# A norm in front of an expert layer, moved from normalized columns to token rows

## The reference, cut to what matters

```python
x = x + gt_a * (merged @ w_o)                       # the products just ahead of the change
h = rms_norm(x, g_ffn) * (1 + sc_f) + sh_f          # factor per feature, shift per feature
logits = h @ w_router + b_router
top_val, top_idx = top_k(logits, 4)                 # 4 of 32
gates = softmax(top_val)
for each expert e, for the tokens xb that chose it:
    u = xb @ w1[e] + b1[e]
    a = min(u[::2], 7) * sigmoid(1.702 * min(u[::2], 7)) * (clip(u[1::2], -7, 7) + 1)
    y += gate * (a @ w2[e] + b2[e])
x = x + gt_f * y                                    # then a last norm
```

## Time and profile before

| what | value |
|---|---|
| median of 3 runs | 1964.3 us (1964.21 to 1966.4) |
| time of the profiled execution | 1965.39 us |
| its span in the trace | 1963.8 us, so 1.6 us lie around it |
| PE / DVE / ACT busy | 94% / 42% / 31% |
| granted PE clock, mean | 0.972 |
| PE share, DMA share of the chain that ended last | 54%, 32% |
| weight transfers of the expert layer | 192 of 2048 KB, through SP |

### The profile page before, as it was taken

How to read it: one execution, slowest core, us unless ns; L and a number is a source line. 1 busy time by engine, 2 the same in 40 slices (tenths; PEclk the granted TensorE clock), 3 DMA queues, 4 the chain that set the end, 5 groups by cost and what they waited for, 6 DMA issues and landing times.

```text
span 1963.8 us, 27025 instructions
## 1 busy us (share of the span) xinstructions
PE 1840.9 (94%) x10839; PEld 1212.9 (62%) x10840; DVE 817.7 (42%) x1402; ACT 612.3 (31%) x996; POOL 27.1 (1%) x49
## 2 busy tenths in 40 slices
PE   6899998989999899999989999999999999999996
PEld 5677777988899799989964444443443443443441
DVE  4466775557864554455532221221221221221222
ACT  4455558645544445555431000000000000000001
POOL 2000000000000000000000000000000000000000
PEclk8998999999999899999969999999999999999998
DMA  6545644455565364534739999999999999999995
GB/s 198 207 169 199 232 131 127 151 164 164 187 207 177 123 216 151 172 129 143 256 151 412 429 429 428 429 429 429 428 429 429 429 428 429 429 429 428 429 429 232
DMA packets 147620, 568.62 MB, mean 290 GB/s; under 512 B 5825, under 2 KB 102185, under 8 KB 122849
## 3 DMA queue, kind: packets, MB, share of 16 engines
q1 hardware_dynamic: 139616, 536.60, 69.3%
q0 software_dynamic: 7936, 31.07, 4.5%
HBM read 566.58 MB, written 3.43 MB: 290 GB/s over the span
## 4 chain that ended last, share of the span: by engine, by line
PE 54%; DMA 32%; DVE 7%; ACT 5%; issue 2%; SPq 0%; DVEq 0%; ACTq 0%
DMA s_ring<-in_w_mlp 31%; PE banks L2034 10%; PE banks L1652 7%; PE banks L1653 7%; PE banks L1654 7%; PE banks L1798 4%; PE banks L2071 3%; PE banks L1799 2%; PE banks L2044 2%; DVE s_W L1135 2%; DVE r_w2l L1097 2%; ACT r_w2h L701 1%; PE banks L1791 1%; PE banks L1619 1%; PE banks L1793 1%
## 5 line engine op out<-in xcount | busy, mean ns | idle before, releaser
L2034 PE MATMUL banks<-s_ring,s_W 128*64 128x512 f32 x2048 | 460.8, 597 | 28.3 <-DMA s_ring<-in_w_mlp 28.3
L2034 PEld LDWEIGHTS banks<-s_ring,s_W 128*64 128x64 f32 x2048 | 139.2, 137 | 330.3 <-issue 259.2
L1037 ACT ACTIVATE s_W<-s_W 128x512 f32<-128x512 f32 x32 | 20.2, 630 | 761.7 <-DVE s_W L1535 761.7
L2071 PE MATMUL banks<-s_ring,s_W 128*64 128x512 f32 x1024 | 226.8, 596 | 0.4 <-ACT s_W L1030 0.4
L1527 DVE TENSOR_TENSOR s_W<-banks,s_W 128x512 f32<-128x512 f32 x32 | 22.1, 691 | 461.5 <-PE banks L2071 461.5
L2071 PEld LDWEIGHTS banks<-s_ring,s_W 128*64 128x64 f32 x1024 | 73.4, 138 | 147.9 <-issue 134.1
L1097 DVE TENSOR_TENSOR r_w2l<-s_ring,r_w2h 128x1024 fp32r<-128x1024 f32 x88 | 107.6, 1223 | 114.0 <-ACT r_w2h L701 113.5
L1311 DVE TENSOR_TENSOR r_w2l<-s_ring,r_w2h 128x1024 fp32r<-128x1024 f32 x96 | 116.9, 1223 | 84.3 <-ACT r_w2h L885 84.1
L1514 DVE TENSOR_TENSOR s_W<-banks,s_W 128x512 f32<-128x512 f32 x128 | 82.1, 683 | 146.8 <-PE banks L2019 146.8
L1652 PE MATMUL banks<-r_x2h,r_w2h 128*128 128x256 f32 x448 | 130.6, 292 | 6.1 <-DVE r_x2l L1325 6.1
L2044 PEld LDWEIGHTS banks<-s_W 128*128 128x128 f32 x1024 | 120.0, 196 | 24.2 <-issue 24.2
(11 more groups left out here) (399 smaller groups left out, 3131.5 us busy)
## 6 DMA issues: line engine op xcount, KB each, us to landing
s_ring<-in_w_mlp SPq DMA_DIRECT2D x192, 2048.0 KB, 22.4
s_ring<-in_w_in SPq DMA_DIRECT2D x62, 1024.0 KB, 5.1
s_W<-in_w_ada POOLq DMA_DIRECT2D x6, 2048.0 KB, 10.0
s_ring<-in_w_ada POOLq DMA_DIRECT2D x6, 2048.0 KB, 8.7
s_ring<-in_w_ffn_gate SPq DMA_DIRECT2D x11, 1024.0 KB, 5.4
s_ring<-in_w_ffn_up SPq DMA_DIRECT2D x11, 1024.0 KB, 7.9
s_ring<-in_w_ffn_down SPq DMA_DIRECT2D x5, 2048.0 KB, 8.7
s_ring<-in_w_gate SPq DMA_DIRECT2D x8, 1024.0 KB, 5.4
```

The lines of the kernel that those rows point to most:

```text
L2034: last = mm(pb[b][64 * h:64 * h + 64, :], XgT[:, 2 * c + k, :], slot(c, 2)[:, k, 1024 * h + 512 * b:1024 * h + 512 * b + 512], start=False ...
L2071: last = mm(pb[2][64 * h:64 * h + 64, :], aT[:, k, 64 * c:64 * c + 64], slot(4 + c, 4)[:, k, 512 * h:512 * h + 512], start=c == 0 and k == ...
```

## The change

The normalized `hn` is no longer made. The router works on raw x: its weights are multiplied by the gain factor once (`wrg`), the shift's share of the logits is one row that is added to the router bias (`wrs`, `wsum`), and 1/rms is a factor per token, so it is applied after the product, on token rows. These preparations are two new steps `wrA` and `wrB` inside the `o` stage. The sum of squares is now made per token (`token_square`: x squared as the stationary side, a column of ones as the moving side), and the router product of a block (`logits`) stands between the `o` products too. ACT takes the root with Sqrt, whose table is loaded during the stage.

Raw x is turned once to token rows; ACT multiplies by the token's factor as it copies to `htok`; the turned raw x stays in banks 4 to 7 for the first sum. The gain factor and the shift are applied to the gathered tokens: the copy of bank 3 to `XgT` becomes eight activations of 64 columns, each with a factor column and a shift column read from SBUF (`modulated_rows`), in every expert. The semaphore `xg` is raised by the eighth. The four rounds that built `msk` and `gat` become one comparison over 256 columns and one reduction each, and the first sum with all that belongs to it (`first_sum`) stands behind the products of expert 0.

```diff
+                 (unit_of("o"), 1, 1, {"wrA": 1.5, "wrB": 2.5}))
...
+        def modulated_rows():
+
+            for k in range(KT):
+                last = act.activation(XgT[:, k, :], pb[3][:, 64 * k:64 * k + 64], ACT.Identity,
+                                      bias=mod_at[:, k:k + 1], scale=mod_at[:, 8 + k:9 + k])
+            return last
...
                 act.wait_ge(S["gath"], e + 1)
                 since(act, "u_mm", e * 4)
-                act.activation(XgT, pb[3].rearrange("p (a n) -> p a n", a=KT), ACT.Copy).then_inc(S["xg"], 1)
+                modulated_rows().then_inc(S["xg"], 1)
...
-        root(4, nrms, T)
-        for t in range(KT):
-            act.wait_ge(S["norm_x"], 4 * KT + t + 1)
-            act.activation(hn[:, t, :], hn[:, t, :], ACT.Identity, bias=modT[:, 24 + t:25 + t]).then_inc(S["norm_s"], 1)
+        act.wait_ge(S["norm_ms"], 5)
+        act.activation(root4, pb[3][:, 0:2], ACT.Sqrt, bias=epsc, scale=1.0 / D).then_inc(S["norm_r"], 1)
...
-        norm(4, hn, hx, nrms, gsf)
-
-        dve.wait_ge(S["moe_in"], 48)
...
+        st.do(tt(one4, iotae.unsqueeze(1).unsqueeze(1).broadcast_to([P, 2, 4, E]), at, ALU.is_equal))
+        st.wait()
+        nc.vector.tensor_reduce(msk, one4.rearrange("p t j e -> p t e j"), AX.X, ALU.add).then_inc(S["route"], 1)
...
+        def logits(k):
...
+            last = mm(pb[5][0:E, 0:T], wrg[:, k, :], hx[:, k, :], start=k == 0, stop=k == KT - 1)
...
+        def token_square(k):
+
+            if k >= 1:
+                logits(k - 1)
+            if k == KT - 1:
+                logits(k)
+            pe.wait_ge(S["norm_sq"], KT * 4 + k + 1)
+            for t in range(2):
+                last = mm(pb[3][:, t:t + 1], nsq[:, k, P * t:P * t + P], ones[:, 0:1], start=k == 0 and t == 0, stop=k == KT - 1, skip_group_check=True)
...
         expert(0, True, False)
-
+        first_sum()
         pe.wait_ge(S["acc_init"], 4)
```

More of the change, by code:

```diff
@@ L980, in _ @@
                 act.activation(v, v, ACT.Sigmoid).then_inc(S["gab_done"], 1)
+                if h == 3:
+                    act.activation(sml[:, 48:49], onec, ACT.Sqrt)
             elif s == "rgS":
@@ L1004, in _, with first_sum @@
             act.activation(half.rearrange("q (c k p) -> q c p k", c=2, k=2), pb[4 + b].rearrange("q (c p k) -> q c p k", c=2, k=2),
[L1005 to L1009, removed]
-        act.activation(gts, gts, ACT.Exp).then_inc(S["log_exp"], 1)
[L1011 to L1019, removed]
+                           ACT.Copy, scale=rtok[:, b // 2:b // 2 + 1]).then_inc(S["ht_kept"], 1)
+        act.wait_ge(S["route"], 3)
+        act.activation(gts, gts, ACT.Exp).then_inc(S["log_exp"], 1)
+        def first_sum():
+            for b in range(2):
+                act.wait_ge(S["spread"], b + 1)
+                act.activation(gtb[:, 512 * b:512 * b + 512], pb[3 - b], ACT.Copy).then_inc(S["spread_kept"], 1)
+            act.wait_ge(S["spread_kept"], 2)
+            for b in range(2):
+                v = slice(64 * b, 64 * b + 64)
+                act.activation(gty[v, :], gtb[v, 512 * b:512 * b + 512], ACT.Copy).then_inc(S["spread_kept"], 1)
+            act.wait_ge(S["gt_mm"], 1)
+            act.activation(gatT, pb[2][0:E, 0:T], ACT.Copy).then_inc(S["gt_kept"], 1)
+            for b in range(4):
+                act.wait_ge(S["h_mm"], b + 1)
+                act.activation(acc[:, b // 2, 512 * (b % 2):512 * (b % 2) + 512], pb[4 + b], ACT.Copy).then_inc(S["acc_init"], 1)
+        def modulated_rows():
[3 more added lines that the diff above has]
+            return last
         def expert(e, cur, prev):
@@ L1049, in again @@
             act.wait_ge(S["over_pe"], n * 7 + 2)
-            act.activation(XgT, pb[3].rearrange("p (a n) -> p a n", a=KT), ACT.Copy).then_inc(S["over_act"], 1)
+            modulated_rows().then_inc(S["over_act"], 1)
             act.wait_ge(S["over_pe"], n * 7 + 3)
@@ L1418, in _ @@
                     keep2(g)
+            elif s == "wrA":
+                router()
+            elif s == "wrB":
+                router_bias()
             elif s == "toep":
@@ L1439, in _ @@
                 dl_step(s, h)
-        norm(4, hn, hx, nrms, gsf)
-        dve.wait_ge(S["moe_in"], 48)
[L1444 to L1448, removed]
+        dve.wait_ge(S["route_mm"], 2)
+        nc.vector.tensor_copy(lgT, pb[5][0:E, 0:T]).then_inc(S["route"], 1)
+        dve.wait_ge(S["norm_r"], 5)
+        nc.vector.reciprocal(rtok, root4).then_inc(S["tok_r"], 1)
+        dve.wait_ge(S["tok_r"], 1)
+        dve.wait_ge(S["route_mm"], 3)
+        for t in range(2):
+            st.do(stt(lg[:, t, :], pb[1][:, E * t:E * t + E], rtok[:, t:t + 1], brow, ALU.mult, ALU.add))
         st.wait()
@@ L1484, in _, with gates @@
         st.wait()
-        nc.vector.tensor_copy(cnti[0:1, :], cntf[0:1, :]).then_inc(S["rank_done"], 1)
+        def gates():
+            nc.vector.tensor_copy(cnti[0:1, :], cntf[0:1, :]).then_inc(S["rank_done"], 1)
+            dve.wait_ge(S["log_exp"], 1)
+            st.do(nc.vector.tensor_reduce(sml[:, 32:34], gts[:, :, 0:4], AX.X, ALU.add))
+            st.wait()
+            st.do(nc.vector.reciprocal(sml[:, 34:36], sml[:, 32:34]))
+            st.wait()
+            for t in range(2):
+                st.do(ts(gts[:, t, 0:4], gts[:, t, 0:4], sml[:, 34 + t:35 + t], None, ALU.mult))
+            st.wait()
+            st.do(tt(prod4, one4, gts[:, :, 0:4].unsqueeze(3).broadcast_to([P, 2, 4, E]), ALU.mult))
+            st.wait()
+            nc.vector.tensor_reduce(gat, prod4.rearrange("p t j e -> p t e j"), AX.X, ALU.add).then_inc(S["route"], 1)
+            dve.wait_ge(S["route"], 5)
         def u_half(c):
@@ L1556, in _ @@
         choose_b(0)
+        gates()
+        nc.vector.memset(taken, 0.0).then_inc(S["round"], 1)
+        dve.wait_ge(S["round"], 1)
+        dve.wait_ge(S["rank_done"], 1)
         expert(0, True, False)
+        dve.wait_ge(S["spread_kept"], 2)
+        dve.wait_ge(S["b1_in"], 80)
+        tt(b2s, b2s, gtb[0:E, :], ALU.mult).then_inc(S["b2_scaled"], 1)
         dve.wait_ge(S["acc_init"], 4)
```

160 lines of the change are left out of this document (87 added, 73 removed).

## The result

| | before | after |
|---|---|---|
| median | 1965.4 us (6 runs, 1964.2 to 1968.9) | 1977.5 us (6 runs, 1976.4 to 1987.3) |
| ratio | | 1.0073 (95%: 1.0049 to 1.0098) |
| a second series | 1966.1 us | 1979.7 us, ratio 1.0069 (1.0049 to 1.0089) |
| profiled execution, span | 1965.4, 1963.8 us | 1977.8, 1976.2 us |

What follows compares the result with a forecast made beforehand. PE was to replace the transfers as the limit: T 1036.9 plus 898.0 (18.4 + 879.6) gives 1934.9 against 1931.10, 3.8 us later, so 1968.3 us; range 1957 to 1981, the forecast's own 1964 to 1974.

Steps and rivals of the forecast that it cites:

- T: Start of expert 1's products, 1041.62 us before; forecast at 1036.9.
- c: PE's time for each expert in the loop, 27.86 us before; forecast 29.32, with PE the limit above 29.04.
- the price of an activation: Eight activations of bank 3 in each expert: starts 0.28 us apart, 0.39 for the last.
- the hand-over: From the end of ACT's eighth activation to PE's start in each expert: 0.05 us.
- (1): `o` stage: added router products, column pairs and `wrB` matmuls make it 3.5 us longer, last product ending at 981.6.
- (2), (3): From the last `o` product to the gather: logits turned by 984.3, indices, ranks and choice matrix done by 990.3.
- (4): Ahead of the first sum: gather 5.0 us, eight activations 2.5, expert 0's products 14.9.
- (5): From the end of expert 0's products to expert 1's: first sum, gather and activations, 24.2 us, clock falling midway.
- A free second column: Rival: an activation's second column operand is nearly free, the transfers decide the end; 1958.9 us, chance 0.17.
- The clock did not stay up: Judges the rival that PE keeps full clock ahead of expert 1, whose products start at 1027.4; 1958.6 us, chance 0.07.
- the dearer activations: Rival: activations cost 0.05 us more apart, or PE's clock falls at times in the loop; 1980 us, chance 0.16.
- half clock throughout: Rival: half clock through gather, expert 0's products and first sum, expert 1's products at 1041.1; 1972.3 us, chance 0.12.

Runs made afterwards that it cites:

- e4: Kernel before, its one copy of bank 3 replaced by eight plain copies of 64 columns without column operands: 1967.7 us (one run).
- e5: The changed kernel measured again, unaltered: 1979.7 us, ratio to before 1.0069.
- e6: Changed kernel with `xg` raised every second activation, product parts waiting only for their blocks, and first sum back in front of expert 0: 1960.2 us.
- e8: Kernel before, its one copy of bank 3 replaced by eight activations of 64 columns with one column operand: 1969.2 us (one run).
- e3: Kernel before, its one copy of bank 3 replaced by eight activations of 64 columns with two column operands: 1981.2 us, ratio 1.0078.
- e7: Changed kernel with `xg` raised every second activation, product parts waiting only for their blocks, and first sum between experts 15 and 16: 1954.9 us.

## Why the prediction came out as it did

Direction, mechanism and place were right: T and c are the two numbers that matter, PE takes the end over from the transfers, the eight activations are the reason. Both numbers were too small, so that 3.8 us were forecast where 12 (between the medians) to 14 (from M) came. The forecast also stands on the first profile's M: from M it was T - M = 1036.9 - 955.95 = 80.9 and end - T = 898.0. Measured were 84.7 and 904.6. With the 3.8 us of the sum this closes: 3.8 + 3.8 + 6.6 = 14.2, against 14.0 between the profiles. The step that was off most is c, 29.32 forecast and 29.54 measured: L2104 is 1.68 us late in each expert, not 1.46. It has two parts, the price of an activation and the hand-over.

- **The bounds of c: right.** 29.04 as the point where PE takes over, and T + 889.5 for the transfers, fit four periods, 27.86, 28.09, 28.81 and 29.54. The point itself is only enclosed, between 28.81 and 29.53.
- **The price of an activation: 0.295 apart and 0.42 for the last, not 0.28 and 0.39.** That is 2.48 us for the eight instead of 2.35. The price of the first column rounded up (0.08 to 0.09) was the right idea; the plain copy was 0.112 apart, where e4 expected 0.11. The prediction shows no row for its slope of 0.85 ns a column; copies of 512 and of 64 columns, 0.49 and 0.112 apart, give 0.84. Times 30 the price is 0.13 x 30 = 3.9 of the 6.6 us. By the Trainium skill, "ScalarE: Activation LUTs", section "What ACT_TABLE_LOAD costs", a column operand costs 93 ns. By this rule, the trace agrees (0.091 and 0.092). The 0.33 apart that an estimate from the page's figures gave was too high here (0.295), since plain neighbours of 64 columns start 0.112 apart. An estimate from the page's 186, 53 and 93 ns gives 0.146 for these.
- **The hand-over: 0.13, not 0.05.** I took the step from PE to DVE for that from ACT to PE. So the copy before had not 0.3 but 1069.41 - 1069.07 - 0.13 = 0.21 us to spare, and e4 bears it out (1.04 - 0.60 - 0.21 = 0.23 late, period 28.09). That is 0.08 x 30 = 2.4 us: a term that is multiplied by 30 was taken from a hand-over between two other engines. Both parts together are 0.21 us an expert, 6.3 of the 6.6 us.
- **(1) the `o` stage: 4.3 us longer instead of 3.5** (26.4 from first to eighth eviction against 22.1). A router product and a pair of columns take 0.55 and 0.54 in the chain, where a square was 0.43; I had 0.43 and 0.48. The unedited part hid this in the raw times.
- **(2), (3): right.** 8.74 us from the eviction of the last product to the gather (980.04 to 988.78), forecast 8.7.
- **(4) 24.0 instead of 22.4:** the gather took 5.64 (5.0), the products 15.76 (14.9), because the half clock began earlier than in the middle of the gather and lasted some 3.6 us into the products.
- **(5) 25.6 instead of 24.2:** the clock was half from the first wide matmul on, not from the middle. It is nearly the 25.7 worked out for half clock. But this is one execution: in e5, the same kernel, (4) took 25.6 and (5) 21.8, since the clock was back for the gather (4.06 in the chain, 6.73 in the first profile). So of the 3.8 us that T - M was off, 2.1 are scatter between two profiles. By its own terms a fall in the middle of the work gives 5.25 for the gather and 23.9 for (5), where 5.0 and 24.2 stand; these nearly cancel.
- **"Expert 0 sooner is worth little by itself": shown** by e6 within its scatter, T - M 78.7 in either order, end - M 2 to 5 us later with the sum ahead.
- **The rivals.** A free second column fell with e8 and e3. The clock did not stay up. The time is nearest to the dearer activations (1980), but not for their reason: the price of 0.295 lies nearer to the forecast's 0.28 than to their 0.33, and the clock in the loop stayed at 1.00 in spite of 1.6 us of idle PE in each expert. T comes near that of half clock throughout (955.95 + 84.7 = 1040.6, against 1041.1), in part for the longer `o` stage. The stated range held the time because it reached to these rivals, which is in part luck; the forecast's own range of 1964 to 1974 did not.

## What to carry to other kernels

When one wide copy in front of products becomes many small ones, count the small ones at their distance, and raise the semaphore for each share that a consumer reads: the same eight activations cost 15 us in the loop behind one wait and, within 1 us, nothing behind four. Find out which side sets the pace of a loop and by how much: 1.18 us of slack in an expert were free, the next 0.5 cost 15 us over 30 experts, and work ahead of such a loop can move into it, in pieces shorter than the transfers on the way: here a period 14.7 us longer than PE needs left no gap in them, one 15.9 longer a gap of some 2.5 us, and one 21.4 longer 8 us. Compare traces from the last mark that the edit cannot have touched.

## What the hardware showed that I had not expected

- A column operand of an activation costs 0.09 us, the first like the second, in duration (0.08) and in distance: 64 columns from PSUM start 0.112, 0.203 and 0.295 us apart with none, one and two.
- Two one-column matmuls of fp32 with 128 stationary columns take 0.54 us in the chain, more than one of 256 columns (0.43).
- Between experts, waits of PE of 1.52 and 0.46 us with the small and wide matmuls between them stood ahead of a fall to 0.50 (e7), while one wait of 1.6 us in each expert of the changed kernel left the clock at 1.00 (1060 to 1940).
- The unedited part ahead of the stage ends anywhere from 950.8 to 966.2 us, and the runs of one kernel scatter by 10 us with it.
